# Block turns on VectorE for half of the cached key pages in a forgetting-attention decoder step

## What is computed

```python
s = jnp.einsum('nqhd,nkhd->nhqk', q, k) * (HEAD_DIM ** -0.5)
s = s + (fq[:, :, :, None] - fk[:, :, None, :])
p = jax.nn.softmax(jnp.where(mask, s, -jnp.inf), axis=-1)
return jnp.einsum('nhqk,nkhd->nqhd', p, v)
```

## Time and profile before

| | us |
|---|---|
| median of 3 runs | 965.12 |
| lowest, highest | 964.96, 965.85 |
| the profiled execution | 964.84 |
| its span in the trace | 963.0 |

### The profile page before, as it was taken

One profiled execution on the slowest core, in us unless ns is written; L12 is line 12 of the kernel. 1 busy time (PEld: TensorE's weight loads), 2 busy tenths in 40 slices (PEclk: granted clock), 3 DMA queues, 4 the chain that ended last, 5 costly groups with the idle time before them and its releaser, 6 DMA issues.

```text
span 963.0 us, 23705 instructions
## 1 busy us (share of the span) xinstructions
PE 931.7 (97%) x8516; PEld 800.4 (83%) x8516; DVE 492.6 (51%) x1133; ACT 383.9 (40%) x728; POOL 163.0 (17%) x111
## 2 busy tenths in 40 slices
PE   4999999999999999999999999999999999999998
PEld 4999999999998997868778778688687787776898
DVE  5775555556345334463554554544545545535632
ACT  5333333322135443553543544535444445345210
POOL 2233333332030221102002012011020020000000
PEclk9999999999999999999999999999999999999999
DMA  7233322224343516889799799798996997987412
GB/s 235 67 88 87 87 70 83 81 72 118 127 153 115 174 57 201 284 292 351 239 367 332 238 385 302 264 380 257 329 348 233 371 328 240 383 297 254 142 44 99
DMA packets 133333, 206.41 MB, mean 214 GB/s; under 512 B 8847, under 2 KB 91456, under 8 KB 133170
## 3 DMA queue, kind: packets, MB, share of 16 engines
q1 hardware_dynamic: 121602, 198.35, 60.8%
q10 hardware_dynamic: 11168, 5.51, 2.1%
q0 software_dynamic: 528, 2.10, 0.8%
HBM read 195.29 MB, written 10.63 MB: 214 GB/s over the span
## 4 chain that ended last, share of the span: by engine, by line
PE 80%; DMA 6%; DVE 4%; ACT 3%; SPq 3%; issue 3%; ACTq 0%; DVEq 0%
PE psum L1221 41%; PE psum L1201 16%; PE psum L1270 9%; PE psum L1404 7%; DMA page_ring<-in_cache_k 4%; PE psum L1519 2%; ACT sample_scores L707 2%; SPq L375 2%; SPq L377 1%; DMA w_raw<-in_a_w_out 1%; PE psum L1447 1%; DMA residual<-in_x_prompt 1%; PE psum L1319 1%; PE psum L1427 1%; DMA page_ring<-in_cache_v 1%
## 5 line engine op out<-in xcount | busy, mean ns | idle before, releaser
L1221 PE MATMUL psum<-xn_high,w_high 128*128 128x256 f32 (+1 forms) x992 | 236.4, 317 | 2.6 <-DVE w_low L832 2.6
L1221 PE MATMUL psum<-xn_low,w_high 128*128 128x256 f32 (+1 forms) x992 | 215.8, 296 | 0.0
L1221 PE MATMUL psum<-xn_high,w_low 128*128 128x256 f32 (+1 forms) x992 | 215.6, 296 | 0.0
L1221 PEld LDWEIGHTS psum<-xn_high,w_high 128*128 128x128 f32 x992 | 163.1, 191 | 16.8 <-issue 13.3
L1221 PEld LDWEIGHTS psum<-xn_high,w_low 128*128 128x128 f32 x992 | 168.3, 190 | 0.0
L1221 PEld LDWEIGHTS psum<-xn_low,w_high 128*128 128x128 f32 x992 | 168.2, 190 | 0.0
L1201 PE MATMUL psum<-constants,page_ring 128*128 128x128 f32 x1024 | 136.9, 276 | 3.7 <-DMA page_ring<-in_cache_k 2.4
L1201 PEld LDWEIGHTS psum<-constants,page_ring 128*128 128x128 f32 x1024 | 114.0, 140 | 29.8 <-issue 27.6
L501 POOL TENSOR_TENSOR w_raw<-w_raw,gains 128x1024 f32<-128x1024 f32 x32 | 61.5, 1925 | 338.4 <-DMA w_raw<-in_b_w_in 217.6
L832 DVE TENSOR_TENSOR w_low<-w_raw,w_high 128x1024 fp32r<-128x1024 f32 x32 | 58.2, 1819 | 67.0 <-ACT w_high L565 67.0
L1009 DVE COPY k_turned_odd<-psum 128x512 f32<-128x512 f32 x64 | 44.1, 690 | 93.5 <-PE psum L1201 93.5
(11 more groups left out here) (236 smaller groups left out, 1467.8 us busy)
## 6 DMA issues: line engine op xcount, KB each, us to landing
page_ring<-in_cache_k SPq DMA_DIRECT2D x128, 512.0 KB, 5.8
page_ring<-in_cache_v SPq DMA_DIRECT2D x128, 512.0 KB, 5.2
w_raw<-in_a_w_in SPq DMA_DIRECT2D x30, 512.0 KB, 4.0
suffix<-suffix_scratch SPq DMA_DIRECT2D x32, 256.0 KB, 4.8
w_raw<-in_b_w_in SPq DMA_DIRECT2D x16, 512.0 KB, 6.8
w_raw<-in_kv_w SPq DMA_DIRECT2D x16, 512.0 KB, 6.2
w_raw<-in_a_w_out SPq DMA_DIRECT2D x4, 1024.0 KB, 5.1
f_broad<-f_scratch SPq DMA_DIRECT2D x8, 512.0 KB, 6.3
```

The costliest lines, as they stand in the source:

```text
L1221: mm = pe.matmul(PS[:, bank + h, 0:c.stop - c.start], w[:, k, :], x[:, k, c], start=(k == 0 and n == 0), stop=(k == KT - 1 and n == 2))
```

## The change

K pages 0 to 7 of a pass are no longer turned by TensorE. VectorE transposes each in place in the ring, one instruction over 128x1024 that transposes every 32x32 block by itself. The keys then lie along the free axis, in four groups by 32-row block, and a slice of 32 partitions holds 32 of a head's 64 dimensions. `block_units` scores all eight pages in one unit: for each of 8 slices, 4 column tiles and 4 row tiles, a 32x32 matmul over 256 columns, 128 in all, row tile r into bank C0 + r (C0, C1, OP, OS). Its stationary operand `q_blocks` holds the queries by 32 dimensions. A new step ahead of the loop lays the queries out by quarters (16 matmuls, four copies), and GpSimd fills `q_blocks` and `q_current` for each sequence; `q_spread` is filled at the end only. VectorE adds the suffix to the unit in two instructions of 128x512 (`add_suffix_blocks`).

The key order of these pages differs, so V pages 0 to 7 are loaded with their rows in that order (still 4 KB a row), and the suffix sums of those pages are stored from a second copy in that order (`suffix_rows`).

The order of a pass changes. TensorE does projection 0 whole, `block_units`, three pieces of projection 1, then pages 8 to 15 as before with the other five pieces and three units. VectorE turns pages 0 and 1 before the gating of the pass ahead, 2 and 3 behind it, 4 to 6 at the start of the pass, then copies k, then turns page 7. SP loads suffix, f and weights at the head of a pass; pages 8 to 15 wait for `b_su`, the end of the unit, and V pages 0 to 7 for the turns of pages 8 to 15. The norm's sums move from behind page 9 to behind page 13.

The core of the diff; counts that only change with the number of turns (24 to 16) and of units (8 to 6) a pass are left out:

```diff
@@ -374,7 +377,11 @@
...
             src = (kpages if n < NPG else vpages)[bass.ds(page, 1), :, :]
-            sp.dma_start(ring[:, n % RING, :], src.rearrange("a p n -> (a p) n")).then_inc(b_page[n % RING], 16)
+            if NPG <= n < NPG + BLK:
+                src = src.rearrange("a (r n) d -> n (a r) d", r=4)
+            else:
+                src = src.rearrange("a p n -> (a p) n")
+            sp.dma_start(ring[:, n % RING, :], src).then_inc(b_page[n % RING], 16)
@@ -401,23 +408,24 @@
...
                 if n == 0:
...
+                    for c in range(2):
+                        load_suffix(i, c)
+                    sp.wait_ge(b_split, KT + 3 * i + 2)
+                    load_w(wqz, (i + KT) * P, 1)
...
                     sp.dma_start(FB[:, :, :], src).then_inc(b_fb, 16)
-                    sp.wait_ge(b_split, KT + 3 * i + 2)
-                    load_w(wqz, (i + KT) * P, 1)
-                if n == 4 and not last:
-                    sp.wait_ge(b_split, KT + 3 * i + 1)
-                    load_w(wkv, (i + 1 + KT) * P, 0)
+                    if not last:
+                        sp.wait_ge(b_split, KT + 3 * i + 1)
+                        load_w(wkv, (i + 1 + KT) * P, 0)
+                if n in (8, 10):
+                    c = 2 + (n - 8) // 2
+                    sp.wait_ge(b_suf, 2 * i + c - 1)
+                    load_suffix(i, c)
...
                     load_w(wkv, (i + 1) * P, 1)
-                if n in (4, 8, 12, 16):
-                    c = n // 4 + 1
-                    if not (last and c >= 4):
-                        sp.wait_ge(b_c1f, 8 * i + n // 4)
-                        load_suffix(i + c // 4, c % 4)
@@ -428,8 +436,11 @@
...
                     sp.wait_ge(s_table, 16 * 3)
-                    if n < NPG:
-                        sp.wait_ge(b_t1, 24 * i + n + 1)
+                    if n < BLK:
+                        if n == 0:
+                            sp.wait_ge(b_su, i + 1)
+                    elif n < NPG:
+                        sp.wait_ge(b_t1, 16 * i + n - BLK + 1)
@@ -488,8 +500,9 @@
...
         for b in range(NB):
-            pool.dma_start(suffix_dram[b].rearrange("h (g n) -> g h n", g=NPG),
-                           CS[b * NPG:(b + 1) * NPG, :, :]).then_inc(s_sfx_st, 16)
+            to = suffix_dram[b].rearrange("h (g n) -> g h n", g=NPG)
+            pool.dma_start(to[0:BLK], CSP[b * NPG:b * NPG + BLK, :, :]).then_inc(s_sfx_st, 16)
+            pool.dma_start(to[BLK:NPG], CS[b * NPG + BLK:(b + 1) * NPG, :, :]).then_inc(s_sfx_st, 16)
@@ -502,9 +515,27 @@
...
             scale_b(n % 2, n // 2 + 1, G_B if n < KT else G_KV)
+        def block_queries(b):
+            own = QN[:, bass.ds(b, 1), 0:2 * H * NQ].rearrange("p a (j x f q) -> p x (a j) f q", x=4, f=2, q=NQ)
+            to = QD[:, :, :].rearrange("p (j x f) n -> p x j f n", x=4, f=2)
+            for x in range(4):
+                pool.tensor_copy(to[:, x, :, :, NQ * x:NQ * x + NQ], own[:, x]).then_inc(b_qc, 1)
+            for e in range(2):
+                h = slice(64 * e, 64 * e + 64)
+                pool.wait_ge(b_qc, 8 * b + 4 + 2 * e)
+                for z in range(2):
+                    c = 16 * z + 8 * e
+                    pool.tensor_copy(QC[h, :, :].rearrange("p (j z) n -> p z j n", z=2)[:, z, :, c:c + NQ],
+                                     QF[h, :, bass.ds(SEQ + b * NQ, NQ)].rearrange("p (j z) q -> p z j q", z=2)[:, z]
+                                     ).then_inc(b_qc, 1)
...
         pool.wait_ge(q_out, KT)
-        pool.tensor_copy(QC[:, :, :], QZ[:, 0, :, :]).then_inc(b_qc, 1)
         pool.tensor_copy(QT[:, :], QF[:, 0, 0:SEQ]).then_inc(b_qt, 1)
+        pool.wait_ge(s_qne, 4)
+        pool.wait_ge(s_zero, 2)
+        block_queries(0)
@@ -514,16 +545,27 @@
...
                 scale_b(1, 7 + 2 * i, G_KV)
...
-                pool.tensor_copy(QC[:, :, :].rearrange("p k n -> p (k n)"),
-                                 QZ[:, bass.ds(i + 1, 1), :, :].rearrange("p a k n -> p (a k n)")).then_inc(b_qc, 1)
+                block_queries(i + 1)
...
+        pool.wait_ge(b_t0, 16 * NB - 4)
+        pool.wait_ge(b_t1, 16 * NB - 4)
+        pool.memset(QZ[:, :, :, :], 0.0).then_inc(m_qz, 1)
...
@@ -661,31 +711,25 @@
...
-            for k in range(NPG):
+            pr, sa = both(D0)
+            act.wait_ge(b_proj, KT + 3 * i + 1)
+            act.wait_ge(b_gl, i)
+            act.wait_ge(b_ddve, i + 1)
+            act.activation(prompt2(SQ[:, 0:SEQ]), pr, ACT.Square)
+            act.activation(SQ[:, SEQ:TOK], sa, ACT.Square).then_inc(b_dact, 1)
+            for k in range(NPG - BLK):
...
                 if k % 2 == 0 and k >= 4:
...
                         PS[:, T0, :].rearrange("p (k n) -> p k n", k=4)).then_inc(b_t0f, 1)
-                if k == 6:
-                    pr, sa = both(D0)
-                    act.wait_ge(b_proj, KT + 3 * i + 1)
-                    act.wait_ge(b_gl, i)
-                    act.wait_ge(b_ddve, i + 1)
-                    act.activation(prompt2(SQ[:, 0:SEQ]), pr, ACT.Square)
-                    act.activation(SQ[:, SEQ:TOK], sa, ACT.Square).then_inc(b_dact, 1)
-                if k == 10:
+                if k == 1:
                     high_b(KT + 3 * i + 2, 1)
-                if k == 14:
-                    pr, sa = both(D0)
-                    act.wait_ge(b_proj, KT + 3 * i + 2)
-                    act.activation(prompt2(VT[:, 0:SEQ]), pr, ACT.Copy)
-                    act.activation(VT[:, SEQ:TOK], sa, ACT.Copy).then_inc(b_dact, 1)
-                if k == 9:
+                if k == 5:
@@ -693,6 +737,10 @@
...
                     act.activation(RR[:, :], RR[:, :], ACT.Exp, scale=-0.5).then_inc(b_rr, 1)
+                if k == 6:
+                    act.wait_ge(b_proj, KT + 3 * i + 2)
+                    act.activation(prompt2(VT[:, 0:SEQ]), pr, ACT.Copy)
+                    act.activation(VT[:, SEQ:TOK], sa, ACT.Copy).then_inc(b_dact, 1)
@@ -926,6 +974,9 @@
...
         dve.wait_ge(s_rtot, 1)
+        dve.tensor_tensor(CSP[:, :, :].rearrange("p h (n r) -> p h r n", r=4),
+                          PS[:, 7, 0:H].unsqueeze(2).unsqueeze(3).to_broadcast([P, H, 4, 32]),
+                          CS[:, :, :].rearrange("p h (r n) -> p h r n", r=4), ALU.subtract)
@@ -989,7 +1031,22 @@
...
         dve.tensor_copy(FQN[:, :, :], PS[:, T0, 128:128 + QB * H].rearrange("p (t h) -> p t h", h=H)).then_inc(s_fnr, 1)
+        def turn_pages(i, ks):
+            for k in ks:
+                dve.wait_ge(b_page[k], (4 * i + 1) * 16)
+                dve.transpose(ring[:, k, :], ring[:, k, :]).then_inc(b_kt, 1)
+        turn_pages(0, range(2))
         query(KT - 1, 1)
+        turn_pages(0, range(2, 4))
+        def quarters(c):
+            out = QN[:, :, 0:2 * H * NQ].rearrange("p b (m c q) -> p c m b q", c=4, q=NQ)[:, c]
+            return out, PS[:, T0 + c, :].rearrange("p (m b q) -> p m b q", b=NB, q=NQ)
+        dve.wait_ge(s_qn, 1)
+        for c in range(2, 4):
+            dve.tensor_copy(*quarters(c)).then_inc(s_qne, 1)
@@ -1016,38 +1073,49 @@
...
-            for k in range(NPG):
+            def add_suffix_blocks(c):
+                dve.wait_ge(b_sfx[c], (2 * i + 1) * 16)
+                dve.wait_ge(b_su, i + 1)
+                dve.memset(TINY[0:1, 32 + c:33 + c], 0.0)
+                out, later = (z.rearrange("p (m r) -> p r m", r=4) for z in (SS[:, c * 512:(c + 1) * 512], SFX[:, c, :]))
+                dve.tensor_tensor_reduce(out, PS[:, C0:OS + 1, c * P:(c + 1) * P], later, 1.0, NEG, ALU.add, ALU.max,
+                                         TINY[:, 6 + c:7 + c]).then_inc(b_suf, 1)
+            turn_pages(i, range(4, 7))
+            dve.wait_ge(b_proj, KT + 3 * i + 1)
+            pr, sa = both(D0)
+            gk = GAIN[:, G_K:G_K + 1]
+            dve.tensor_scalar(prompt2(KN_T[:, 0:SEQ]), pr, gk, None, ALU.mult)
+            dve.tensor_scalar(KN_T[:, SEQ:TOK], sa, gk, None, ALU.mult).then_inc(b_ddve, 1)
+            turn_pages(i, range(7, 8))
+            for c in range(2):
+                add_suffix_blocks(c)
+            for k in range(NPG - BLK):
...
                 if k % 2 and k >= 3:
-                    u = k // 2 - 1
+                    u = 4 + k // 2 - 1
...
                         dve.wait_ge(b_sfx[(u // 2) % 2], (2 * i + u // 4 + 1) * 16)
-                    dve.wait_ge((b_c0, b_c1)[u % 2], 8 * i + u // 2 + 1)
-                if k == 6:
-                    dve.wait_ge(b_proj, KT + 3 * i + 1)
-                    pr, sa = both(D0)
-                    gk = GAIN[:, G_K:G_K + 1]
-                    dve.tensor_scalar(prompt2(KN_T[:, 0:SEQ]), pr, gk, None, ALU.mult)
-                    dve.tensor_scalar(KN_T[:, SEQ:TOK], sa, gk, None, ALU.mult).then_inc(b_ddve, 1)
+                    dve.wait_ge((b_c0, b_c1)[u % 2], 6 * i + (u - 4) // 2 + 1)
...
                 if k % 2 and k >= 3:
-                    add_suffix(k // 2 - 1)
-                if k == 11:
+                    add_suffix(4 + k // 2 - 1)
```

(59 more changed lines are left out.)

121 lines of the change are left out of this document (65 added, 56 removed).

## The result

The changed kernel takes 1064.29 us (median of 4 runs, 1061.95 to 1065.93) against 965.04 for the kernel before, measured beside it (4 runs, 962.05 to 965.85): 1.1031 times the time, interval 1.1008 to 1.1053. The prediction was 990, range 955 to 1028, 0.80 for slower. The sign was right; the time is 74 us over the forecast and outside the range. The profiled execution spans 1060.8 us against 963.0.

The account below looks back on a forecast made before the run. TensorE, 97% busy, bounds the kernel, with DMA engines near their limit. A pass takes 39.1 against 35.7: +3.4, seven times +23.8; first pass +1.4; 963.0 becomes 988.2 of span, plus 1.8: 990 us, range 955 to 1028.

Parts of the forecast that it names:

- Wait ahead of the unit: Between projection 0 and the unit, TensorE stands still 6.9 us until VectorE has turned page 7.
- Its fall of the clock: A TensorE stop of 6.9 us lowers its clock, so the unit costs 2.1 us more, 5.9.
- Page 8 behind the unit: Pages 8 to 15 are issued only when the unit ends; page 8 is there 3.6 us after it.
- rival D: In the unit, row tiles take turns: +11 us a pass, 1078 us in all; chance 0.08.
- V pages and GpSimd's end: V pages wait in the ring as before; GpSimd's last-pass filling of spread queries starts some 20 us ahead of its reader.
- A: TensorE's clock doesn't fall in the stop ahead of the unit: 2.1 us less in seven passes, 975 us; chance 0.15.
- B: VectorE turns at the rate of the 0.81 row, the wait shrinks to 4.2 us, the clock holds: 956 us; chance 0.16.
- C: VectorE's turn costs 1.82 us, or only eight tiles run abreast in the unit (+3.7 a pass): 1020 us; chance 0.18.
- SP now issues both suffix loads, f and two weights at the head of a pass ... so nothing: Head of a pass: five loads come when nothing else can be loaded, ahead of SP's wait for the unit; cost nothing.
- 15 x 0.23 + 0.4 = 3.8 us: The unit at full clock: 256 instructions, sixteen abreast, make sixteen rounds of 0.23 us, 3.8 us.
- I take 0 of the 0 to 2.4: Early in the run, VectorE's second-order suffix subtraction takes 2.4 us, covered by TensorE's four queued output tiles: 0.
- The first pass ... +1.4: Pass 0, where pages are there early: its rewritten stretch ends at 401.9 against 400.5, +1.4 us.

Follow-up runs that it names:

- the run that it changes: Changed kernel with suffix chunks 2 and 3 loaded behind two and five page loads of the pass instead of eight and ten; 1031.12 us, ratio 1.0674.

## Why the prediction was right or wrong

**Right.** VectorE's turn: 1.22 us for 1.2. Wait ahead of the unit: 5.8 to 6.3 us for 6.9 in passes 1 to 7, 2.5 for 2.3 in pass 0. Its fall of the clock: the window at 0.80 and 0.69, and the two runs that filled the wait took it away (unit 7.05 to 5.28 us). Page 8 behind the unit: 702.41 to 706.53 is 4.1 us for 3.6; the first load begins 0.9 us behind the unit (at 703.34), not 0.3. Sixteen tiles abreast: the 256 matmuls take 4.9 us, not the 14.8 of rival D. V pages and GpSimd's end: TensorE waits 3.3 us in all for V pages where it waited 2.2, and the tail is 73.8 us in both. So the mechanisms of the forecast are there, but it put them at 25 us in all, and the change costs 99. Rivals A, B and D fell, and so did C: the turn was 1.2 and the tiles ran abreast.

**Wrong, by size:**

- "SP now issues both suffix loads, f and two weights at the head of a pass ... so nothing" looked at chunks 0 and 1 and never at 2 and 3. This is the step that failed. They go behind eight and ten page loads that themselves wait for the unit, and VectorE waits for chunk 2 ahead of a copy that TensorE needs. 4.2 us of stall in pass 4 and a second clock fall; in all 33 us by the run that loads it early. The kernel before has the same code line (VectorE waits for `b_sfx` ahead of the copy), harmless there because the loads came at 4, 8, 12 and 16. The stall cannot be read from the trace of before; it can be read from the diff, by asking of each queue what stands ahead of each load.
- "15 x 0.23 + 0.4 = 3.8 us" for the unit at full clock. The round of 0.23 came from four column tiles of 128 rows. With 32-row tiles it is 4.9 / 16 = 0.31 (4.9 us from first to last start in passes 1 to 7 where the wait is filled); in pass 0 of the changed kernel 5.5, with a gap of 0.39 in it that no semaphore ends. With the fallen clock 6.1 to 7.4 from first to last start, for 5.9 in all: the whole unit of pass 4 takes 7.05, 1.2 us more. Here I chose the rows against a page, and the page was nearer to the 5.28 us that the whole unit takes at full clock: the Trainium skill (TensorE: Matmul & The Clock Gate, Part 3) had led to 5.6 us.
- "I take 0 of the 0 to 2.4" for the second suffix subtraction. It took 4.00 us, not the 2.4 worked out from the earlier trace rows; the same subtraction in the common order, right behind it (L980), took 2.28, so the permuted order of its operands is what distinguishes it. And it was on the path, two steps on: it holds back the weight split, that holds SyncE's next slab load (asked for at 241.13 us against 237.35), and its landing (251.22 against 246.65) holds TensorE, 6.1 us in place of 1.3. TensorE reaches the sums of the last query (L1390) at 368.15 against some 361.9: 6.3 us. TensorE had output tiles queued, but the cover was for VectorE's delay and not for the load behind it. In the run without the subtraction the stop is 2.0 us and the sums come at 364.48, 3.4 us earlier than in the run that it changes (367.91). So some 3.4 of the 6.3 are the subtraction's; 2.6 over the kernel before are left without it, with a fall of the clock behind that stop, and what causes them was not tested (sixteen suffix stores in place of eight are one candidate).
- "The first pass ... +1.4" instead of 21.6. 6.3 are there ahead of the last query, as above; the 32 matmuls took 5.19 us for 3.7; the unit (5.9 us for 3.8), the stall of 4.9 us and its clock fall came on top in pass 0 too. I did not test the rest of this sum singly.

Per pass, in pass 4 the stretch to page 15's turns takes 46.7 us for 39.1: wait 6.0 for 6.9, unit 7.1 for 5.9, page 8 at 4.1 for 3.6, and stall with its clock fall 5 to 6 for 0. The other terms are off by less than 0.6 each (projection 0 6.7 for 6.4, the idle time ahead of pages 9 and 10 0.8 for 0.4, the wait ahead of page 15 0.3 for 0.8), and about one microsecond I can't place.

**What the clock does.** TensorE's granted clock is 1.00 in every pass of the kernel before. In pass 4 of the changed kernel it is still near 1.00 until about 693, then 0.50 (the level of 1.2 GHz) to the end of the wait and past the middle of the unit, and 1.00 from 700:

```profile
691.00:693.00 2.00, 0.00 (x0) 0.00 (x0) 2.00 (x3) 0.00 (x0) 0.00 (x0) 0.97 1.08 254
693.00:694.00 1.00, 0.00 (x0) 0.00 (x0) 1.00 (x4) 0.14 (x1) 0.00 (x0) 0.50 1.19 258
...
700.00:701.00 1.00, 1.00 (x69) 0.96 (x55) 0.00 (x0) 0.00 (x0) 0.67 (x1) 1.00 0.00 0
```

By the rule the forecast drew on (the Trainium skill, TensorE: Matmul & The Clock Gate, HAM oscillation) each burst behind a long wait starts at the low clock: the trace agrees, 0.69 over the unit. The length of the stop alone does not tell whether the clock falls, though. The wait of 2.5 us in pass 0 leaves it at 1.00, while in the run without the subtraction it fell behind the stop of 2.0 us that ends at 252.32:

```profile
250.00:252.30 2.30, 0.32 (x3) 0.12 (x1) 2.30 (x3) 0.00 (x0) 2.19 (x1) 1.00 0.26 29
...
254.00:256.00 2.00, 2.00 (x11) 2.00 (x11) 0.00 (x0) 0.00 (x0) 0.00 (x0) 0.50 1.07 378
```

Filling the wait ahead of the unit with six matmuls restores 13 us, and 9 with the early suffix.

## What to carry to other kernels

Work moved between engines also moves the moment at which buffers come free. Here a third of the loss, the suffix load's 33 us, and the wait ahead of the unit lay on one chain: pages land one by one, VectorE turns them, one unit needs all eight, eight loads wait for the unit, and the suffix waits behind those loads. Follow each queue (and each engine's program order) from the moved step to the next stop; a stage that takes its inputs one by one as they land has cover that a batch of eight hasn't.

When a wait can't be removed, work put into it gives back what the fallen clock costs (here 1.8 us in a unit), as long as it ends with the wait: eleven matmuls overran it by 3.6 us and lost more than they gave, six gained. And a wait put in front of an instruction delays all who need that instruction: place it directly in front of the one that reads the data.

## What the runs showed of the hardware that I had not expected

Beyond some length of a loop's body, TensorE pays for its own instructions in each pass. Changed kernel, 785 matmuls a pass (the recorded count), each with a weight load: 22 packets on the instruction queue. 48 more: 23. 64 more: 59, and breaks in some passes. 96 more: 86, and 257 more: 95, with some 5 to 6 us of idle time ahead of the first matmul of a pass and, where the program has the most, up to 2.9 at a time inside the units. A packet is 0.36 MB / 22, 16 KB. The Trainium skill (Runtime: NRT & Kernel Launch, Instruction fetch mechanics) states that TensorE's instruction memory holds 2048 instructions, is refilled in blocks of 16 KiB, and that a taken branch whose target isn't in the current window of two blocks waits for a fetch. The traces agree in kind: 785 matmuls and as many loads are 1570 instructions, and with 64 more pairs 1698, before waits and register instructions are counted; the count at which it breaks is shown only between 48 and 96 more pairs. They don't agree with a window of two blocks: at the 256 instructions a block of that section the changed kernel's pass is some six blocks (an estimate), and its loop runs with 22 packets in the whole execution.

A round of sixteen 32x32 tiles takes 0.31 us with 256 columns and 3.3 / 16 = 0.21 with 128: it is neither bound by issue alone nor by columns alone.
